# Order of the table lines in the mixers and of the shared rows in the summing stage, and half of the shared expert moved to the end of the experts' stage

## What is computed

```python
# first block, once: three mixers, each with its own columns of w_in
cols = split_columns(rms_norm(x) @ w_in)
o_a = nsa_mixer(cols, ..., rel_bias[:, :8])   # 8 heads, table of relative bias
o_b = swa_mixer(cols, ..., rel_bias[:, 8:])   # a second table
o_c = fox_mixer(cols, ...)
...
# second block, two layers: mixer, then a mixture of experts
scores = sigmoid(xt @ router_w)               # 64 experts, top 8 of each token
for each block of tokens of one expert e:
    hb = silu(xb @ w_gate[e]) * (xb @ w_up[e])
    yb = (hb @ w_down[e]) * weight
routed = segment_sum(yb)
shared = (silu(xt @ ws_gate) * (xt @ ws_up)) @ ws_down   # inner width 256
x = layer_norm(ALPHA * x + gate2 * (routed + shared))
```

## Time and profile before

| | |
|---|---|
| median of 3 runs | 3659.82 us (3649.41 to 3661.64) |
| the profiled execution: its time | 3663.34 us |
| the profiled execution: its span, first to last instruction | 3661.5 us |
| mean granted TensorE clock | 0.931 of full speed |
| PE busy | 3239.2 us, 88% |
| DVE, ACT, POOL busy | 44%, 27%, 6% |
| HBM read, written | 722.76 MB, 58.72 MB |
| mixer A's projections | 61 to 202 us |
| mixer C's projections | to 546 us |
| routing ends | about 1744 and 2942 us |
| experts end | about 2411 and 3584 us |
| summing starts | 2413 and 3586 us |

### The profile page before, as it was taken

The page is one execution under the profiler, slowest core; times in us unless marked ns, Lnnn a source line. Parts: engine busy times, 40 slices in busy tenths (PEclk is TensorE's granted clock), DMA queues, the critical chain, the costliest instruction groups (busy, mean ns, idle before and its releaser), DMA issues. The chain is left out here.

```text
span 3661.5 us, 46618 instructions
## 1 busy us (share of the span) xinstructions
PE 3239.2 (88%) x14519; PEld 2083.2 (57%) x14520; DVE 1610.3 (44%) x4117; ACT 983.0 (27%) x2061; POOL 218.2 (6%) x212
## 2 busy tenths in 40 slices
PE   4889899997999988998899999977989889899895
PEld 2565566875878755876444444455677644444444
DVE  2246546665656446445332333253734523323235
ACT  2336435223323235322111111113532211111110
POOL 0000000000000000000111111100000011111111
PEclk8969899998999999997999999988999899999997
DMA  2210113663454240223899999953022289999985
GB/s 101 88 58 1 70 26 99 180 213 115 135 193 142 82 134 16 78 72 123 345 408 399 401 403 400 390 216 122 10 76 80 85 354 414 402 397 395 393 353 224
DMA packets 287704, 750.26 MB, mean 205 GB/s; under 512 B 25948, under 2 KB 167646, under 8 KB 231365
## 3 DMA queue, kind: packets, MB, share of 16 engines
q1 hardware_dynamic: 234564, 630.52, 45.2%
q0 software_dynamic: 27648, 67.51, 4.7%
q10 hardware_dynamic: 25344, 50.33, 4.1%
HBM read 722.76 MB, written 58.72 MB: 213 GB/s over the span
## 5 line engine op out<-in xcount | busy, mean ns | idle before, releaser
L2736 PE MATMUL up_ps<-experts,x_turned 128*64 128x512 f32 (+1 forms) x2256 | 700.1, 625 | 94.7 <-DMA experts<-in_w_up_dram 76.0
L263 DVE TENSOR_TENSOR pieces_lo<-weights,pieces_hi 128x512 fp32r<-128x512 f32 (+1 forms) x468 | 316.0, 684 | 512.3 <-ACT pieces_hi L257 511.4
L2736 PEld LDWEIGHTS up_ps<-experts,x_turned 128*64 128x64 f32 (+1 forms) x2256 | 269.5, 161 | 453.8 <-issue 443.8
L257 ACT CAST pieces_hi<-weights 128x512 fp32r<-128x512 f32 (+1 forms) x468 | 284.1, 614 | 577.8 <-PE gate_ps L275 167.1
L2760 PE MATMUL y_ps<-experts,hid_turned 128*64 128x512 f32 (+1 forms) x1128 | 345.7, 601 | 1.6 <-ACT hid_turned L2816 1.6
L2883 DVE TENSOR_TENSOR hid_seats<-up_ps,gated 128x256 f32<-128x256 f32 x94 | 57.4, 611 | 578.1 <-ACT gated L2809 578.1
L273 PE MATMUL gate_ps<-h_hi,pieces_hi 128*128 128x512 f32 x624 | 249.1, 399 | 32.2 <-DVE pieces_lo L263 32.2
L273 PE MATMUL products<-h_hi,pieces_hi 128*128 128x512 f32 x464 | 203.7, 439 | 68.0 <-DVE pieces_lo L263 68.0
L275 PE MATMUL gate_ps<-h_hi,pieces_lo 128*128 128x512 f32 x624 | 246.5, 395 | 0.0
L274 PE MATMUL gate_ps<-h_lo,pieces_hi 128*128 128x512 f32 x624 | 246.4, 395 | 0.0
L2760 PEld LDWEIGHTS y_ps<-experts,hid_turned 128*64 128x64 f32 (+1 forms) x1128 | 117.4, 154 | 222.2 <-issue 222.2
(11 more groups left out here) (443 smaller groups left out, 5085.6 us busy)
## 6 DMA issues: line engine op xcount, KB each, us to landing
experts<-in_w_gate_dram SPq DMA_DIRECT2D x141, 1024.0 KB
experts<-in_w_up_dram SPq DMA_DIRECT2D x141, 1024.0 KB
experts<-in_w_down_dram SPq DMA_DIRECT2D x141, 1024.0 KB, 17.1
ada_weights<-in_w_ada_dram ACTq DMA_DIRECT2D x48, 1024.0 KB, 5.3
rows_sb<-results SPq DMA_DIRECT2D x16, 2048.0 KB, 25.1
weights<-in_w_in_dram SPq DMA_DIRECT2D x57, 512.0 KB, 4.2
weights<-in_w_in_dram SPq DMA_DIRECT2D x12, 2048.0 KB, 10.4
weights<-in_w_out_dram SPq DMA_DIRECT2D x6, 2048.0 KB, 8.4
```

The lines of the kernel that those rows point to most:

```text
L257: act.copy(self.like(view, self.hi[:, i % self.BUFFERS, :, :]), view).then_inc(s["hi_ready"], 1)
L263: dve.tensor_tensor(lo, view, hi.bitcast(F32), ALU.subtract).then_inc(s["lo_ready"], 1)
L2736: made = pe.matmul(up_ps[part, b, :].rearrange("p (h n) -> p h n", h=2), xT[:, b, k, part], experts.up(b + i)[:, :, k, :], start=(k == 0), ...
```

## The change

1. In `project_heads` ACT keeps table line h two steps later (step first + h + 2) and fills its edge in step first + h + 3. The second table starts one step earlier (first = 11). A semaphore `edge_ready` makes the second table's first line wait for the first table's eight fills. PE's spread of the root rows waits until the last table's lines are kept. DVE's `scale` and ACT's copy of a turned tile move one step later, and the loops run one or two steps longer.
2. In `route_tokens` only the products for features 0 to 127 are left. Two of their 16 matmuls come after the turned plan; then come find 0 and find 1, with no product between or behind them.
3. In `routed_experts`, behind the last down product, PE makes the 16 matmuls for features 128 to 255 into the two `up_ps` banks, ACT the silu, DVE the product. `hT_e` and `shared_up` stay allocated until then.
4. In `combine`, `shared(t + 1)` comes before `back(t - 1)`.

```diff
@@ -514,8 +515,8 @@
...
         self.at_turn = {2 * j + 3: v for v, (j, sources, dst, gate) in enumerate(turned)}
-        self.at_keep = {2 * j + 4: v for v, (j, sources, dst, gate) in enumerate(turned)}
-        self.end = 1 + max([self.n_pieces, self.at_reciprocal] + [max(x) for x in (self.at_scale, self.at_keep) if x])
+        self.at_keep = {2 * j + 5: v for v, (j, sources, dst, gate) in enumerate(turned)}
+        self.end = 2 + max([self.n_pieces, self.at_reciprocal] + [max(x) for x in (self.at_scale, self.at_keep) if x])
@@ -579,6 +580,8 @@
...
                     pe.wait_ge(s["rstd_ready"], 1)
+                    for table in made[-1:]:
+                        pe.wait_ge(table.sem(s, "line_ready"), H)
@@ -648,10 +651,10 @@
...
                     for table in made:
-                        if table.first <= i < table.first + H:
-                            table.keep(act, s, i - table.first, spread)
-                        if table.first + H <= i < table.first + 2 * H:
-                            table.fill(act, s, i - table.first - H)
+                        if table.first + 2 <= i < table.first + 2 + H:
+                            table.keep(act, s, i - table.first - 2, spread)
+                        if table.first + 3 <= i < table.first + 3 + H:
+                            table.fill(act, s, i - table.first - 3)
@@ -679,7 +682,7 @@
...
                         dve.reciprocal(rstd[:, :], root[:, :]).then_inc(s["rstd_ready"], 1)
-                    for n in when.at_scale.get(i, ()):
+                    for n in when.at_scale.get(i - 1, ()):
@@ -692,12 +695,12 @@
...
-    NAMES = ("table_loaded", "filled", "line_spread", "line_ready", "written", "read")
+    NAMES = ("table_loaded", "filled", "line_spread", "line_ready", "edge_ready", "written", "read")
...
         self.width = tables.shape[2]
-        self.first = 1 + (H + 3) * order
+        self.first = 1 + (H + 2) * order
@@ -741,13 +744,14 @@
...
             act.wait_ge(s[f"written_{self.order - 1}"], 16)
+            act.wait_ge(s[f"edge_ready_{self.order - 1}"], H)
...
             act.activation(self.tables[:, h, 0:self.width - 256], self.prog.zeros[:, 0:self.width - 256], ACT.Identity,
-                           bias=self.line[:, h, 0:1])
+                           bias=self.line[:, h, 0:1]).then_inc(self.sem(s, "edge_ready"), 1)
@@ -2222,7 +2226,7 @@
...
-def route_tokens(prog, experts, passes, late_norms, mod, xT, rw, rb, shared_down, shared_down_loaded,
+def route_tokens(prog, experts, passes, late_norms, mod, xT, rw, rb, shared_up, shared_down, shared_down_loaded, hT,
@@ -2233,8 +2237,6 @@
...
     with ExitStack() as ctx:
-        hT = prog.sb(ctx, "hT_e", [P, DK, T])
-        shared_up = prog.sb(ctx, "shared_up", [P, 2, DK, FF])
@@ -2249,7 +2251,7 @@
...
         NONE = -3e38
-        silu = prog.sb(ctx, "silu", [P, 2, T])
+        silu = prog.sb(ctx, "silu", [P, T])
@@ -2269,7 +2271,7 @@
...
         plan_ps = banks[:, 0, :].rearrange("p (i n) -> p i n", i=4)
-        shared_ps = [[banks[:, 6 - 2 * m + j, :] for m in range(2)] for j in range(2)]
+        shared_ps = [banks[:, 6 + j, :] for j in range(2)]
@@ -2339,16 +2341,12 @@
...
-                def shared_product(j, m, hook=False):
-                    for k in range(DK):
-                        if hook and k == 5:
-                            pe.wait_ge(s["plan_ready"], 1)
-                            e = experts_of(pe, 0)[0]
-                            pe.wait_ge(s["matched"], 1)
-                            passes.find(pe, 0, e, info, find_ps[0]).then_inc(s["found"], 1)
-                        last = pe.matmul(shared_ps[j][m], shared_up[:, j, k, m * P:(m + 1) * P], hT[:, k, :],
-                                         start=(k == 0), stop=(k == DK - 1))
-                    last.then_inc(s["up_made"] if j else s["gate_made"], 1)
+                def shared_product(j, ks):
+                    for k in ks:
+                        last = pe.matmul(shared_ps[j], shared_up[:, j, k, 0:P], hT[:, k, :], start=(k == 0),
+                                         stop=(k == DK - 1))
+                        if k == DK - 1:
+                            last.then_inc(s["up_made"] if j else s["gate_made"], 1)
@@ -2372,17 +2370,20 @@
...
                 pe.wait_ge(s["shared_loaded"], 32)
-                shared_product(0, 0)
-                shared_product(1, 0)
+                shared_product(0, range(DK))
+                shared_product(1, range(6))
...
                 last.then_inc(s["plan_turned"], 1)
-                shared_product(0, 1, hook=True)
+                shared_product(1, range(6, DK))
+                pe.wait_ge(s["plan_ready"], 1)
+                e = experts_of(pe, 0)[0]
+                pe.wait_ge(s["matched"], 1)
+                passes.find(pe, 0, e, info, find_ps[0]).then_inc(s["found"], 1)
...
                 passes.find(pe, 1, None, info, find_ps[1]).then_inc(s["found"], 1)
-                shared_product(1, 1)
@@ -2404,9 +2405,8 @@
...
                              banks[:, i % 2, :].rearrange("p (a k) -> p a k", k=DK)).then_inc(s["h_copied"], 1)
-                for m in range(2):
-                    act.wait_ge(s["gate_made"], m + 1)
-                    act.activation(silu[:, m, :], shared_ps[0][m], ACT.Silu).then_inc(s["silu_ready"], 1)
+                act.wait_ge(s["gate_made"], 1)
+                act.activation(silu[:, :], shared_ps[0], ACT.Silu).then_inc(s["silu_ready"], 1)
@@ -2418,11 +2418,6 @@
...
-                def shared_hidden(m):
-                    dve.wait_ge(s["silu_ready"], m + 1)
-                    dve.wait_ge(s["up_made"], m + 1)
-                    dve.tensor_tensor(hid[:, m, :], shared_ps[1][m], silu[:, m, :], ALU.mult)
@@ -2584,11 +2579,12 @@
...
                     passes.keep_notes(dve, b, b, find_ps[b]).then_inc(s["noted"], 1)
-                shared_hidden(0)
-                shared_hidden(1)
...
-def routed_experts(prog, experts, passes, seat, info, plan, base):
+                dve.wait_ge(s["silu_ready"], 1)
+                dve.wait_ge(s["up_made"], 1)
+                dve.tensor_tensor(hid[:, 0, :], shared_ps[1], silu[:, :], ALU.mult)
...
+def routed_experts(prog, experts, passes, seat, info, plan, base, shared_up, hT, hid_shared):
@@ -2602,6 +2598,7 @@
...
         y = prog.sb(ctx, "y_seats", [P, 2, D])
+        silu_shared = prog.sb(ctx, "silu", [P, T])
@@ -2609,7 +2606,7 @@
...
                         "up_made_0", "up_made_1", "up_made_2", "silu_ready", "hid_ready", "hid_turned", "hid_copied",
-                        "down_made_0", "down_made_1", "down_made_2", "write_noted", "y_dve", "y_act", "go", "shared_out",
+                        "down_made_0", "down_made_1", "down_made_2", "write_noted", "y_dve", "y_act", "go", "shared_out", "shared_made", "shared_silu",
@@ -2791,6 +2788,12 @@
...
                 down(end, 1)
+                pe.wait_ge(s["hid_ready"], 2 * end + 2)
+                for j in range(2):
+                    for k in range(DK):
+                        last = pe.matmul(up_ps[:, j, :], shared_up[:, j, k, P:2 * P], hT[:, k, :], start=(k == 0),
+                                         stop=(k == DK - 1))
+                    last.then_inc(s["shared_made"], 1)
@@ -2847,6 +2850,8 @@
...
                 weigh(end, 1)
+                act.wait_ge(s["shared_made"], 1)
+                act.activation(silu_shared[:, :], up_ps[:, 0, :], ACT.Silu).then_inc(s["shared_silu"], 1)
@@ -2929,6 +2934,9 @@
...
                 weigh(end, 1)
+                dve.wait_ge(s["shared_silu"], 1)
+                dve.wait_ge(s["shared_made"], 2)
+                dve.tensor_tensor(hid_shared[:, 1, :], up_ps[:, 1, :], silu_shared[:, :], ALU.mult)
@@ -3035,9 +3043,9 @@
...
                     add(t, 1)
-                    back(t - 1)
...
                         shared(t + 1)
+                    back(t - 1)
@@ -3184,9 +3192,11 @@
...
                 passes = Passes(prog, moe)
-                route_tokens(prog, experts, passes, norms, mod, xT, router[:, l, :, :], rb[:, l, :], shared_down, shared_loaded,
-                             hid, sel, seat, info, plan, base)
-                routed_experts(prog, experts, passes, seat, info, plan, base)
+                hT = prog.sb(moe, "hT_e", [P, DK, T])
+                shared_up = prog.sb(moe, "shared_up", [P, 2, DK, FF])
+                route_tokens(prog, experts, passes, norms, mod, xT, router[:, l, :, :], rb[:, l, :], shared_up, shared_down,
+                             shared_loaded, hT, hid, sel, seat, info, plan, base)
+                routed_experts(prog, experts, passes, seat, info, plan, base, shared_up, hT, hid)
```

## The result

The changed kernel takes 3623.5 us (median of 4 runs, 3622.8 to 3626.3), the kernel before, beside it on the same chip, 3660.7 us: a ratio of 0.9905, 95% interval 0.9886 to 0.9923, so 37 us less. The forecast was 3619.4 us in a range of 3604 to 3638. The profiled execution took 3623.76 us with a span of 3622.0, 39.5 us under the span of before.

What follows compares the result with a forecast made beforehand. PE was busy 88% of the span, but mixer A was bound by a PE-ACT-DVE loop and the routing and experts' ends by POOL. Terms 31.1 + 3.7 + 9.2 - 5.6 + 2.0 = 40.4 off 3659.8 gave 3619.4 us, range 3604 to 3638.

Steps and rivals of the forecast that it cites:

- the loop: Mixer A's projections: PE's spread, ACT's copy and rounding, DVE's rest wait on each other; delaying the copy saves 31.1 us.
- PE's own work, 84.3 us: Mixer A: unstalled full-clock time of 20 products, 16 spreads, 8 sums and three turned tiles, from 71 us on.
- The residue of 1.3: Mixer A: 1.3 us of waiting that stays where ACT copies out the two twin tiles.
- The rival that the clock stays low: Mixer A: spreads might not hold the clock, so A gives only 20 us, total 3630.6; chance 0.13.
- lockstep: Mixer A: ACT held each step until the previous product ends, 7.7 us a step, total 3672; chance 0.02.
- C's 3.7: Mixer C: moving DVE's scaling one step later removes two gaps, 2.4 us, and a slow product's excess, 1.3 us.
- (c): Routing: second gather follows find 1, then a 9.0 us DRAIN; stage ends 4.6 us earlier, two layers 9.2 off.
- (b): Routing: find 1 follows the selection's end at once, some 4.6 us earlier per layer, no products standing before it.
- (a): Routing: two of 16 matmuls move behind the turned plan, bringing plan, loads and selections 1.74 us earlier per layer.
- weights decide the drain: Routing: the drain ends with the seven weight loads, so only 1.74 us a layer comes, total 3625; chance 0.13.
- The tails: Experts' stage ends: 16 added matmuls make DVE end instead of POOL, costing 2.6 and 3.0 us, 5.6 in all.
- The summing stage: First summing stage: shared rows replace PE's 1.01 us wait before `back`, twice, 2.0 us off.

Runs made afterwards that it cites:

- tables_only: The kernel before with only mixer A's table-line edits (kept two steps later, filled the step after, second table one step earlier, their two waits): 3631.1 us, ratio 0.9901.
- w9: The changed kernel with nine expert weight loads issued before the end of routing instead of seven: 3616.6 us (one run).
- w2d: The changed kernel with two of seven weight loads left in routing and the first two down loads ahead of the waiting up load: 3619.7 us, ratio 0.9866.
- w4: The changed kernel with four of seven weight loads left in routing, the other three first on SP in the experts' stage: 3613.3 us, ratio 0.9870.
- mixers: The changed kernel with routing and the experts' stage as in the kernel before: 3620.5 us, ratio 0.9897.
- one_step: The changed kernel with table lines kept one step later instead of two, and filled two steps later: 3630.2 us (one run).

## Why the prediction was right or wrong

**Mixer A: mechanism right, term too small by 2.7.** The line copy held ACT, one step of delay breaks the loop, and the clock came back. The stretch lost 33.8 us where 31.1 were forecast; the other 0.9 of the stage's 34.7 lie before and behind it. The stretch was to take 84.3 + 1.3 = 85.6 us and took 82.7, and "PE's own work, 84.3 us" is the part that was mis-sized. It took 16 spreads at their shown duration, 0.91, but a spread takes 0.84 from start to start (74.41 - 70.57 = 3.84, less a product of 3.00): 1.2 too much. It took 0.67 for each turned tile, half of a row of eight transposes, where four take 0.4 from start to start: 0.8 too much. The 20 products were 0.5 too high in all. The residue of 1.3 came out as one gap of 0.96. The rival that the clock stays low fell, and so did lockstep.

**Mixers B and C.** C's 3.7 was forecast for its two gaps and the slow product, and these came: 2.4 of gaps and 1.4 of the product. The stretch lost only 2.6, because the stage's last 3.50 us of before took 4.78, at a granted clock of 0.61 in place of 0.99; the forecast had no term for that. Over all profiles the stretch takes 137.7 to 140.0 us with the change and 140.8 and 144.9 without. B's 2.1 is not an edit of the change that I can point to: the changed code gave 157.0, 163.7 or 166.9 us there (below), and tables_only, whose code there is that of before, gave 163.7 where the kernel before has 165.9.

**Routing: the step that failed is (c), "the DRAIN of 9.0 us behind that; the stage ends 4.6 earlier".** Gather 1 did come earlier, by 4.1 and 5.3 us for 4.6. Of this (b) is shown: the distance between the gathers is 3.1 to 4.9 us in every profile with the old order of PE and 1.4 or 1.5 in every one with the new. Step (a), 1.74 a layer, is not clear of scatter: the first weight load starts 0.9 and 1.7 us earlier in this profile, but 59.1 to 63.8 us into the stage over all profiles with the new order and 61.7 to 63.9 with the old.

But the 9.0 was read as a fixed price of a drain, from four places that agree within 1.4 us. In routing it is the landing time of a gather within the weight stream, 8.7 us, and gather 1 now comes 1.5 instead of 4.7 us behind gather 0, so that both share the engines with the weights at once: 11.9. From gather 0's issue to gather 1's landing the pair takes 13.4 and 13.5 us before and 12.7 and 12.1 after, so 3.2 and 3.6 us of a shorter distance were worth 0.6 and 1.4. With the 0.9 and 1.7 by which gather 0 starts earlier these make the 1.6 and 3.1 that the stages gained.

The rival "weights decide the drain" had the right size, 1.74 a layer, for a wrong reason, as w9 shows. And the row that spoke against it, drains just as long with no load behind them, was of another kind: the experts' drains are 7.911 and 7.577 us, the same in every profile, whatever the loads do, while those of routing went from 4.4 to 12.1. Instructions of one name and nearly one length were taken for one cause. The forecast's total was not hurt, and that is luck: mixer A gave 3.6 us more than its term, routing 4.5 less.

**The tails: right.** +2.8 and +3.1 for 2.6 and 3.0, with DVE as the end and PE's idle time down from 14.7 to 3.5 us.

**The summing stage: mechanism right, its size not shown.** -2.8 for -2.0. The trace shows the two waits of 1.01 us gone. From the stage's first PE instruction to the next stage's first product 9 of the 12 profiles with the new order take 71.4 to 73.0 us, three 75.7 to 76.1; the two with the old order take 75.1 and 76.8. Profiles of one order differ by more than the 2 us, so what the missing waits were worth is not shown.

**Untouched stretches** moved by 0.8 in all, single ones by up to 2.0 (the second attention, 259.44 to 261.48).

Not tried: the scaling and the turned tiles' copies alone, and the summing order alone, each without the other edits. Their shares rest on the stages' own times.

## What to carry to other kernels

A copy that an engine makes in the same step in which another engine produces its input ties the two into one loop; one step of delay frees it, and here the delayed copies alone (tables_only, two steps) gave 34 of the 37 to 40 us. Before a wait's length is carried over to a new order, ask what fills it: a gather beside a stream of loads has no fixed duration. Here two gathers beside seven loads ended 12 to 13.5 us after the first was issued, almost wherever the second one began; what shortened them was fewer loads beside them. Work moved under a cover should be cut to the cover: 8 products fitted beneath POOL's end of stage and were free, 16 stuck out by 3 us.

## What the runs showed of the hardware that was not expected

- Two gathers of up to 128 rows, the second issued 1.5 us after the first, land in 4.3 and 5.2 us on idle DMA engines (w2d), both in 6.5 beside four loads of 1 MB (w4), and in 9.2 and 11.2 beside seven (the changed kernel). Issued 4.7 us after the first, the second one takes 8.7 beside seven (before).
- POOL's DRAIN at the end of the experts' stages took 7911 and 7577 ns in all profiles, to the nanosecond. The Trainium skill (VectorE: DVE Perf Modes, section "The DRAIN you can't avoid") gives about 12 ns for a program's standing DRAINs; these are neither that nor, like routing's, the landing of a transfer beside loads. What they do, no row shows.
- The same code of attention A and mixer B's projections took 157.0 us in three profiles (granted clock 0.93 in the run mixers), 163.6 to 164.1 in six (0.89 in the changed kernel) and 166.9 in three (0.87 in one_step); what puts it in one or another the profiles don't show. The steps between these (3 and 7 us) are as large as most terms of the forecast, so a term of 2 or 3 us in such a stretch is not shown by one profile.
